# Another order of an expert's intermediate units, so that its second weight matrix arrives in larger pieces

## The chip, the cores and the metric

The kernel runs on one core of a Trainium2 chip, in one launch. The metric is the time on the device in microseconds (us).

## The reference, cut to what matters

Two blocks follow each other on 256 tokens of 1024 features, in float32. The first has two layers of a mixer (attention, convolution, stick breaking attention) and a mixture of experts; the second has two layers of another mixer. The change is in the experts of the first block:

```
N_EXPERTS = 64; TOP_K = 8; EXPERT_FF = 256          # D_MODEL = 1024, SEQ = 256

def swiglu(x, w1, w3, w2):
    return (jax.nn.silu(x @ w1) * (x @ w3)) @ w2     # w1, w3: 1024 x 256; w2: 256 x 1024

    def expert_block(args):                          # for each block of tokens sent to expert e
        toks, e, wts = args
        out = swiglu(xpad[toks], w1[e], w3[e], w2[e])
        return out * wts[:, None].astype(out.dtype)
```

Each expert has 256 intermediate units: columns of w1 and w3, rows of w2. The sum over the units in the second product may take them in any order.

## The kernel before

SBUF has 128 partitions. The tokens of an expert are handled in blocks of 64 slots, a list of blocks with their experts being made on the chip after the router. Each layer first runs one block per expert and then the extra ones; the loop takes four blocks (`UNROLL`) a turn, as two pairs (`PAIRS`).

For a block `j` TensorE does, in the order that `pair` writes out by hand:
- `gather` (L1186): picks the tokens of the next pair by a product with a one-hot matrix in bf16, in halves, between the other products.
- `block_h` (L1198): the first product. The contraction runs over the 1024 features, `KT` = 8 tiles of 128. The stationary operand is `x_blk`, 128 features by 64 slots; the moving one is the weights in the ring `w13(j)`, for each feature 256 columns of w1 and 256 of w3. With 64 slots only half of the array's columns are used, so the units are split into two halves `g`, which go to two column tiles side by side: tile 0 writes partitions 0 to 63 of `h_bank`, tile 1 partitions 64 to 127. In the bank, columns 0 to 127 are the w1 part and 128 to 255 the w3 part. A float32 product of the program is two instructions in the trace.
- `block_turn` (L1207, L1210, L1212): the activation `act_blk` (slots of both halves on the partitions, 128 units across) is turned by TensorE. Afterwards partition p holds unit p of half 0 in columns 0 to 63, and unit p of half 1 in columns 64 to 127 (`turned`).
- `pair_w2` (L1225): the second product, for the two blocks of a pair on two column tiles: `turned` stationary, `w2_slots` moving, 512 columns, half `f` of the units from the slot's part `f`.
- `pair_add` (L1238): the weighted results, split into three bf16 parts, are added to the tokens' sums in PSUM.

ScalarE makes the sigmoid (L1488) and copies; VectorE multiplies (L1956, L1958) and applies the norm to the gathered tokens (L1948, L1950).

SP issues all weights by DMA: `expert13` (L670) loads w1 and w3 of an expert into a ring slot, with one contiguous piece of 8192 bytes per partition each (the eight features of a partition lie together), and `expert2` (L675) loads w2 into one of four `w2_slots`, which lie in the tensors `slots2`, `qk` and `z`. In the loop SP waits until block_h has read the ring slot of the last turn (`h_done`), issues expert13, then waits until pair_w2 has read the w2 slot (`o_done`, L797), and issues expert2. So each load has about one turn of the loop less its issue delay before it is read.

Of the kernel before, what the change touches and what calls it, by code (L numbers as in the profile page):

```python
# [31 lines left out]
P = 128  # L32
# [15 lines left out]
N_EXPERTS, N_GROUPS, TOPK_GROUPS, TOP_K, FF = 64, 8, 4, 8, 256  # L48
# [382 lines left out]
def first_block(nc, A, K):  # L431


    ds = bass.ds
    with ExitStack() as ctx:
# [103 lines left out]
        for n in (PAIRS * T * P // 2, FF // 2, FF // 2):  # L539
# [13 lines left out]
        w2_slots = [slots2[:, 0], slots2[:, 1], qk[:].rearrange("p t n -> p (t n)").rearrange("p (f n) -> p f n", f=2),  # L553
                    z_flat[:, 0:T * D].rearrange("p (f n) -> p f n", f=2)]
# [10 lines left out]
        for layer in range(DEPTH):  # L565
            chunks = chunks_1(layer)
            for i, (name, reader) in enumerate(chunks):
                s = i % RING
# [91 lines left out]
        def _(sp):  # L660
# [11 lines left out]
                        .then_inc(w13_filled[s], 16)  # L672

            def expert2(l, e, s):
                sp.dma_start(w2_slots[s], A["w2"][ds(l, 1), ds(e, 1)].rearrange("a b (f p) n -> p (a b f) n", p=P))\  # L675
                    .then_inc(w2_filled[s], 16)

            def load(dst, src, loaded):
# [24 lines left out]
            for l in range(DEPTH):  # L703
# [55 lines left out]
                for e in range(UNROLL):  # L759
# [4 lines left out]
                    else:  # L764

                        sp.wait_ge(B[l][before].full, B[l][before].full_at(l))
                    expert13(l, e, e)
                expert2(l, 0, 0)

                sp.wait_ge(sh_done.sem, sh_done.at(l, T))  # L770
                expert2(l, 1, 1)

                sp.wait_ge(parts_ready.sem, parts_ready.at(l))
                expert2(l, 2, 2)
                expert2(l, 3, 3)
                if l + 1 < DEPTH:
# [57 lines left out]
        def _(pe):  # L834
# [41 lines left out]
            for l in range(DEPTH):  # L876
# [195 lines left out]
                for g in range(4):  # L1072
                    bank = begin(("mT", g), l)
                    for j in range(2):
                        for t in range(T):
                            k = 2 * g + j
# [46 lines left out]
                def w13(s):  # L1123
                    return K.slots[s].rearrange("p (i k) n -> p i (k n)", i=2).rearrange("p i (k n) -> p i k n", n=FF)
# [66 lines left out]
                def block_h(it, j):  # L1191


                    pe.wait_ge(w13_filled[j], uses(it, j // 2) * 32)
                    own = slice(j % 2 * SLOTS, (j % 2 + 1) * SLOTS)
                    for k in range(KT):
                        for g in range(2):
                            mm = nc.tensor.matmul(h_bank[g * SLOTS:(g + 1) * SLOTS, 0:FF], x_blk[:, j // 2, k, own],  # L1198
                                                  w13(j)[:, :, k, g * (FF // 2):(g + 1) * (FF // 2)],
                                                  start=(k == 0), stop=(k == KT - 1), skip_group_check=True)  # L1200
                    mm.then_inc(h_done, 1)

# [40 lines left out]
                def pair(it, i, first=False, last=False):  # L1243
                    a, b = 2 * i, 2 * i + 1

                    pe.wait_ge(x_ready, nth(it, b))
                    block_h(it, a)
                    if not last:
                        gather(it, i + 1, 0)
                    if not first:  # L1250

                        pe.wait_ge(o_rest_ready, nth(it, b - 2))
                    block_turn(it, a)
                    block_h(it, b)
                    if not last:
                        gather(it, i + 1, 1)

                    pe.wait_ge(turned_ready, nth(it, a))
                    pe.wait_ge(weight_ready, pairs(it, i))
                    block_turn(it, b)  # L1260
                    if not first:
                        pair_add(it, i - 1)

                    pe.wait_ge(turned_ready, nth(it, b))
                    if not last:

                        pe.wait_ge(x_ready, nth(it, b + 2))
                    pair_w2(it, i)
# [1492 lines left out]
```

## Time and profile before

| | |
|---|---|
| time, median of 3 runs | 2237.6 us |
| lowest and highest | 2233.91 and 2243.11 us |
| the profiled execution | 2242.32 us |
| its span, first to last instruction | 2240.6 us |
| mean granted TensorE clock in it | 0.985 |
| DMA packets, bytes | 165286, 599.13 MB |

The span is the time in which instructions ran; the profiled execution's own time holds 1.7 us more. Engines are called PE (TensorE's products), PEld (its weight loads), DVE (VectorE), ACT (ScalarE), POOL and SP. Durations of matmuls include their way through the array, so instructions that follow each other overlap in the trace; the distance between starts is the rate.

### The profile page before, as it was taken

How to read it: one execution, taken by the hardware profiler on the slowest of the kernel's cores; microseconds unless marked ns; L12 is line 12 of the kernel's file. 1: busy time of each engine (PE TensorE's matmuls, PEld its weight loads, DVE VectorE, ACT ScalarE, POOL GpSimd, SP SyncE). 2: the span in 40 equal slices, each digit the busy share in tenths (PEclk: the TensorE clock that was granted, in tenths of full speed). 3: DMA queues.
4: the chain of work that ended last, by engine and by line, in shares of the span. 5: the costliest groups of instructions: out<-in, count | busy, mean ns of one | idle time of the engine just before them, and what ended most of it. 6: DMA issues, size and time to landing. Idle time of an engine off the chain costs nothing. (4 is left out here: it accounts for less than half of the span.)

```text
span 2240.6 us, 34873 instructions
## 1 busy us (share of the span) xinstructions
PE 2132.4 (95%) x13404; PEld 1232.9 (55%) x13404; DVE 973.5 (43%) x2062; ACT 510.0 (23%) x1077; POOL 59.7 (3%) x143
## 2 busy tenths in 40 slices
PE   5999999899999999979999988999999999799998
PEld 3844444556556565557454445556565565367475
DVE  2673423544444444428634244444444443353153
ACT  2223112122222222223231111222222222113131
POOL 1000002000000000000000030000000000100000
PEclk9999999999999999989999999999999999899999
DMA  9652838699999999845527437999999998531721
GB/s 325 203 206 75 300 113 319 224 385 376 385 378 382 386 379 381 341 179 179 198 105 260 167 130 279 380 382 381 383 378 389 377 386 286 178 111 57 225 69 56
DMA packets 165286, 599.13 MB, mean 267 GB/s; under 512 B 13052, under 2 KB 17760, under 8 KB 130656
## 3 DMA queue, kind: packets, MB, share of 16 engines
q1 hardware_dynamic: 163808, 595.10, 70.7%
q0 software_dynamic: 1408, 3.10, 0.7%
q8 instruction: 44, 0.72, 0.1%
q14 instruction: 26, 0.21, 0.0%
HBM read 597.11 MB, written 1.05 MB: 267 GB/s over the span
## 5 line engine op out<-in xcount | busy, mean ns | idle before, releaser
L1198 PE MATMUL banks<-weight_ring,h_t 128*64 128x256 f32 x4224 | 481.8, 381 | 3.2 <-DVE h_t L1950 3.2
L1198 PEld LDWEIGHTS banks<-weight_ring,h_t 128*64 128x64 f32 x4224 | 298.3, 137 | 174.0 <-issue 38.2
L849 PE MATMUL banks<-weight_ring,h_t 128*128 128x512 f32 x768 | 335.8, 593 | 4.1 <-issue 1.6
L849 PEld LDWEIGHTS banks<-weight_ring,h_t 128*128 128x128 f32 x768 | 145.1, 190 | 187.6 <-issue 182.8
L1976 DVE SCALAR_TENSOR_TENSOR conv_t<-banks,slot_weight,xn 128x512 f32<-128x512 f32 x132 | 99.1, 751 | 293.5 <-ACT xn L1503 293.5
L1186 PEld LDWEIGHTS banks<-z,sp_ 128*128 128x128 bf16 x3168 | 178.8, 98 | 55.8 <-issue 49.3
L1186 PE MATMUL banks<-z,sp_ 128*128 128x128 bf16 x3168 | 201.0, 220 | 4.9 <-DVEq L1940 4.9
L1238 PE MATMUL banks<-xn,conv 128*128 128x512 bf16 x792 | 185.9, 385 | 6.7 <-issue 4.0
L1503 ACT ACTIVATE xn<-banks,slot_weight 128x512 bf16<-128x512 f32 x132 | 90.7, 687 | 342.6 <-PE banks L1225 342.6
L1956 DVE TENSOR_TENSOR z<-banks,z 128x128 f32<-128x128 f32 x132 | 38.5, 292 | 230.0 <-ACT z L1488 230.0
L2209 PE MATMUL banks<-weight_ring,h_t 128*128 128x512 f32 (+2 forms) x384 | 134.1, 509 | 2.9 <-ACTq L2385 2.9
L1238 PEld LDWEIGHTS banks<-xn,conv 128*128 128x128 bf16 x792 | 78.6, 100 | 89.9 <-issue 9.8
L1225 PE MATMUL banks<-slots,conv 128*64 128x512 f32 x544 | 124.2, 598 | 3.1 <-DVE h_t L1950 3.1
L859 PE MATMUL banks<-h_t,weight_ring 128*128 128x256 f32 x512 | 116.3, 391 | 6.1 <-DVEq L1555 4.5
L1948 DVE TENSOR_TENSOR h_t<-banks,mod_col 128x512 f32<-128x512 f32 x132 | 91.4, 692 | 65.2 <-PE banks L1186 65.2
L1225 PE MATMUL banks<-qk,conv 128*64 128x512 f32 x256 | 116.7, 598 | 0.0
L1225 PE MATMUL banks<-z,conv 128*64 128x512 f32 x256 | 116.7, 598 | 0.0
L859 PEld LDWEIGHTS banks<-h_t,weight_ring 128*128 128x128 f32 x512 | 100.4, 197 | 21.1 <-DVEq L1555 4.6
L1488 ACT ACTIVATE z<-banks 128x128 f32<-128x128 f32 x132 | 36.6, 278 | 327.0 <-PE banks L1198 327.0
L2209 PEld LDWEIGHTS banks<-weight_ring,h_t 128*128 128x128 f32 x384 | 69.0, 190 | 63.5 <-issue 58.4
L1602 DVE SCALAR_TENSOR_TENSOR conv<-hpad,vec_t,conv 128x256 f32<-128x256 f32 x240 | 100.3, 480 | 4.7
L1950 DVE TENSOR_TENSOR h_t<-h_t,mod_col 128x512 f32<-128x512 f32 x132 | 91.4, 692 | 9.8
(467 smaller groups left out, 2045.2 us busy)
## 6 DMA issues: line engine op xcount, KB each, us to landing
weight_ring<-in_w SPq DMA_DIRECT2D x264, 1024.0 KB, 10.9
weight_ring<-in_w_in SPq DMA_DIRECT2D x36, 2048.0 KB, 11.5
slots<-in_w SPq DMA_DIRECT2D x68, 1024.0 KB, 8.5
weight_ring<-in_w_mod SPq DMA_DIRECT2D x24, 2048.0 KB, 10.0
qk<-in_w SPq DMA_DIRECT2D x32, 1024.0 KB, 7.0
z<-in_w SPq DMA_DIRECT2D x32, 1024.0 KB, 11.4
weight_ring<-in_w_out SPq DMA_DIRECT2D x8, 2048.0 KB, 7.8
weight_ring<-in_w_in SPq DMA_DIRECT2D x10, 1024.0 KB, 7.7
```

The costliest lines, as they stand in the source:

```text
L849: mm = nc.tensor.matmul(bank[:, 0:cols], stationary[:, k, t * P:(t + 1) * P], w[:, k, 0:cols], start=(k == 0), stop=(k == KT - 1))
L859: mm = nc.tensor.matmul(bank[:, j * SEQ:(j + 1) * SEQ], w[:, k, c * P:(c + 1) * P], K.h_t[:, k, :], start=(k == 0), stop=(k == KT - 1))
L1186: mm = nc.tensor.matmul(x_banks[half][:, kk * P:(kk + 1) * P], xn_parts[:, t, c, half * KT // 2 + kk, :], pick_hot[:, i % PAIRS, t, :], st ...
L1198: mm = nc.tensor.matmul(h_bank[g * SLOTS:(g + 1) * SLOTS, 0:FF], x_blk[:, j // 2, k, own], w13(j)[:, :, k, g * (FF // 2):(g + 1) * (FF // 2)],
L1225: mm = nc.tensor.matmul(o_banks[h][b * SLOTS:(b + 1) * SLOTS, :], turned[:, i, b, f * SLOTS:(f + 1) * SLOTS], w2_slots[2 * i + b][:, f, h ...
L1238: mm = nc.tensor.matmul(y_bank[t][h][:], slot_of[:, i % PAIRS, t * P:(t + 1) * P], o_parts[:, c, h * CHUNK:(h + 1) * CHUNK], start=False, ...
L1503: nc.scalar.activation(o_parts[:, 0, col], o_banks[h][:], ACT.Copy, scale=slot_weight[:, i % PAIRS:i % PAIRS + 1])\
L1602: v.scalar_tensor_tensor(conv[:, c, :], hpad[:, c, k:k + SEQ], w, conv[:, c, :], ALU.mult, ALU.add)
L1948: v.tensor_tensor(x, x_banks[half][:].rearrange("p (k s) -> p k s", k=KT // 2), broadcast(mod_col[:, 3, ks], 2, P), ALU.mult)
L1950: v.tensor_tensor(x, x, broadcast(mod_col[:, 2, ks], 2, P), ALU.add).then_inc(x_ready, 1)
L1976: v.scalar_tensor_tensor(o_rest[:, col], o_banks[h][:], own, o_parts[:, 0, col], ALU.mult, ALU.subtract)\
L2209: mm = nc.tensor.matmul(bank[:, 0:cols], stationary[:, k, t * P:(t + 1) * P], w[:, k, 0:cols], start=(k == 0), stop=(k == KT - 1))
```

## The change

Two edits. `expert2` loads w2 so that partition p gets the rows 2p and 2p + 1 (before: p and 128 + p); these lie together in memory, so each partition has one piece of 8192 bytes instead of two of 4096. To match, the moving operand of `block_h` gives tile `g` every second column, starting at `g`, of the 256 columns of w1 and w3 (before: the columns g * 128 to g * 128 + 127). Partition p of `turned` then holds the units 2p and 2p + 1.

```
             def expert2(l, e, s):
-                sp.dma_start(w2_slots[s], A["w2"][ds(l, 1), ds(e, 1)].rearrange("a b (f p) n -> p (a b f) n", p=P))\
+                sp.dma_start(w2_slots[s].rearrange("p f n -> p (f n)"), A["w2"][ds(l, 1), ds(e, 1)].rearrange("a b (p f) n -> p (a b f n)", f=2))\
                     .then_inc(w2_filled[s], 16)
...
                             mm = nc.tensor.matmul(h_bank[g * SLOTS:(g + 1) * SLOTS, 0:FF], x_blk[:, j // 2, k, own],
-                                                  w13(j)[:, :, k, g * (FF // 2):(g + 1) * (FF // 2)],
+                                                  w13(j)[:, :, k, g::2],
                                                   start=(k == 0), stop=(k == KT - 1), skip_group_check=True)
```

## Rows read from the trace of the kernel before

**Rows 1.** The page's busy time of each engine, share of the span, instructions.

```profile
PE 2132.4 (95%) x13404; PEld 1232.9 (55%) x13404; DVE 973.5 (43%) x2062; ACT 510.0 (23%) x1077; POOL 59.7 (3%) x143
```

**Rows 2.** Windows: us, then PE, PEld, DVE, ACT, POOL busy, PE clock, DMA share, GB/s.

```profile
440.00:935.00 495.00, 495.00 (x4384) 293.43 (x4381) 220.93 (x481) 117.22 (x271) 0.00 (x0) 1.00 0.98 382
1390.00:1900.00 510.00, 507.77 (x4474) 299.95 (x4473) 224.79 (x488) 121.16 (x279) 0.00 (x0) 1.00 0.96 372
```

**Rows 3.** PE's waits from 415 to 940 us: total us, times, longest.

```profile
PE banks L1186 <- DVEq L1940: 2.0, 1, 2.0
PE banks L1198 <- DVE h_t L1950: 1.6, 1, 1.6
PE banks L1225 <- DVE h_t L1950: 1.5, 1, 1.5
```

**Rows 4.** PE's groups in the expert stage: out<-moving,stationary, shapes, count | busy us, mean ns.

```profile
L1198 PE MATMUL banks<-weight_ring,h_t 128*64 128x256 f32 x4224 | 481.8, 381 | 3.2 <-DVE h_t L1950 3.2
...
L1207 PE MATMUL banks<-ident,z 128*128 128x128 f32 x132 | 37.1, 281 | 4.8 <-DVE z L1958 4.8
```

**Rows 5.** Order of time on PE: start us, length us, what, count.

```profile
603.14 3.62 PE L1198 MATMUL banks<-weight_ring,h_t 128*64 128x256 f32 x32
...
619.64 2.54 PE L1198 MATMUL banks<-weight_ring,h_t 128*64 128x256 f32 x22
...
632.66 3.65 PE L1225 MATMUL banks<-slots,conv 128*64 128x512 f32 x16
```

**Rows 6.** Streams of other products: two groups, and four column tiles in order of time.

```profile
L849 PE MATMUL banks<-weight_ring,h_t 128*128 128x512 f32 x768 | 335.8, 593 | 4.1 <-issue 1.6 <-DMA weight_ring<-in_w_in 1.6 <-ACTq L1453 0.9
...
L2236 PE MATMUL banks<-h_t,weight_ring 128*128 128x256 f32 x256 | 56.1, 380 | 0.0
...
137.08 1.92 PE L886 MATMUL banks<-weight_ring,c_act 128*32 128x512 f32 x16
```

**Rows 7.** Transposes by line: ns min/median/max. L870 step 8, L1111 step 2, L992 contiguous.

```profile
L870 PEld LDWEIGHTS banks<-ident,xn x16: 185/192/197, 35.3 to 37.2; 128*128 128x128 f32 x16
L870 PE MATMUL banks<-ident,xn x16: 272/274/278, 35.7 to 37.3; 128*128 128x128 f32 x16
...
L1111 PEld LDWEIGHTS banks<-ident,act_h x4: 196/216/262, 1341.5 to 1342.3; 128*128 128x128 f32 x4
...
L992 PEld LDWEIGHTS banks<-ident,xn x32: 138/140/144, 177.1 to 1121.9; 128*128 128x128 f32 x32
```

**Rows 8.** DMA: packets; L675's issue times and landing; SP's wait; SP in time.

```profile
DMA packets 165286, 599.13 MB, mean 267 GB/s; under 512 B 13052, under 2 KB 17760, under 8 KB 130656
...
L675 SPq DMA_DIRECT2D slots<-in_w x68: 378/384/1545, 402.2 to 1874.9; - x68
...
DMA to landing us min/median/max: 4.9/8.6/14.3
...
SPq L797 <- PE banks L1225: 653.2, 62, 11.6
...
605.84 1.53 SPq L675 DMA_DIRECT2D slots<-in_w  x1
```

**Rows 9.** A window (columns as in rows 2) in which loads queue up.

```profile
1343.00:1345.00 2.00, 1.57 (x8) 1.18 (x9) 0.70 (x5) 0.50 (x2) 0.00 (x0) 1.00 1.05 442
```

More of the change, by code:

```diff
@@ L674, in expert2 @@
             def expert2(l, e, s):
-                sp.dma_start(w2_slots[s], A["w2"][ds(l, 1), ds(e, 1)].rearrange("a b (f p) n -> p (a b f) n", p=P))\
+                sp.dma_start(w2_slots[s].rearrange("p f n -> p (f n)"), A["w2"][ds(l, 1), ds(e, 1)].rearrange("a b (p f) n -> p (a b f n)", f=2))\
                     .then_inc(w2_filled[s], 16)
@@ L1198, in block_h @@
                             mm = nc.tensor.matmul(h_bank[g * SLOTS:(g + 1) * SLOTS, 0:FF], x_blk[:, j // 2, k, own],
-                                                  w13(j)[:, :, k, g * (FF // 2):(g + 1) * (FF // 2)],
+                                                  w13(j)[:, :, k, g::2],
                                                   start=(k == 0), stop=(k == KT - 1), skip_group_check=True)
```

## Prediction

> **What bounds the kernel now.** I read the page's busy line first [rows 1]: TensorE is busy for 2132.4 us of the 2240.6 us span, so whatever TensorE does is the candidate. The change touches only the expert stage, so the next view is the windows of that stage [rows 2]. From 440 to 935 us (first layer) TensorE is busy for 495.00 of 495 us, from 1390 to 1900 us (second layer) for 507.77 of 510 us, at a granted clock of 1.00. The same rows show the DMA engines at 98% and 96% of their time, moving 382 and 372 GB/s. Two resources look full; which of them sets the pace must come from the waits. TensorE's waits from 415 to 940 us [rows 3] are three, 5.1 us together, all for VectorE and all at the stage's start. None is for a DMA. The transfers are close to full because they are asked for at just that rate, not because TensorE stands waiting for them.
>
> The groups by line [rows 4] show what TensorE does there. The first product (L1198) is 4224 instructions, 481.8 us; L1207 runs once per block of 64 slots, so there are 132 blocks and 32 instructions of L1198 in each. They go in twos: the two halves of the columns are computed on two column tiles side by side. I call two such instructions a step: 4224 / 2 = 2112 steps, and 481.8 us / 2112 = 228 ns a step, tails included. In the order of time [rows 5] 32 instructions take 3.62 us; without the last one's own length (381 ns), 15 intervals share 3.24 us, 216 ns each. A pair of blocks takes 619.64 - 603.14 = 16.5 us, all of it TensorE's work.
>
> **The change part by part.**
>
> *Moving operand of L1198.* Instruction count, columns per instruction (256), weights loaded and PSUM columns written stay. What changes is that each tile reads every second float of the w1 and w3 rows (a step of 8 bytes) instead of 128 floats in a row. No moving operand of the trace of before reads with a step, so this price is unknown and must be bounded.
> - From below: can a step get shorter? L2236 [rows 6] is the same 256 columns on the whole array, one stream: 56.1 us / 256 = 219 ns. The two tiles (216 to 228 ns) already run at the pace of one stream, so the columns set it, not the reads. Bound: 0.
> - From the reads as they are: how much can the moving side deliver? L886 runs four column tiles with four different streams of 512 floats. Its 16 instructions take 1.92 us [rows 6]; without the last one's 0.59 us, three intervals share 1.33 us, 443 ns for four streams at once. L849 needs 335.8 us / 768 = 437 ns for one stream of the same length. So four contiguous streams cost no more than one. Two streams with a step of two walk over as many bytes per ns as four contiguous ones (each walks over twice what it uses). By this row they fit: price 0.
> - From above: a stepped read does cost something elsewhere. The weight load of the transposes at L870 (a step of 8 floats) takes 192 ns at the median, that of L992 (contiguous, the same 128x128 floats) 140 ns [rows 7]; L1111, with the very step of 2, has a minimum of 196 and a median of 216 ns. L870's own matmuls take 272 to 278 ns, so it was not the clock. That is 52 ns for 128 columns, 0.41 ns a column. Such a load takes 0.41 ns more, but the moving side is slower to begin with: from 380 ns at 256 columns (L2236) to 593 ns at 512 (L849) [rows 6], 0.83 ns a column. If a stepped read can deliver one float each 0.83 ns, the load drops to exactly that and the moving read does not notice. If instead the same 0.41 ns is added per moving column, a step costs 256 x 0.41 = 105 ns more, 2112 x 0.105 = 222 us. If each column took twice its 0.83 ns, it would be 213 ns a step, 450 us.
>
> I take 0. The two rows with the same kind of read and the same rate (L886 for the sum of the streams, L870 for one stream at its slowest) both leave room; the 222 and 450 us need a limit that neither row shows. It is at the edge, though: both fit without slack that I can see.
>
> The Trainium skill, "SBUF — State Buffer", section "Specifications (TRN2)", says that the memory has 16-byte lines and needs at least two accesses in a line for full bandwidth. Floats with a step of two have exactly two in a line, so by that rule the sum stays at 0 for one stream; the page says nothing of two streams that share a line. L870's step of eight, with one access in a line, is slowed by the 52 ns above, which agrees with it; L1111's step of two is slowed as much, which speaks against it. The sums of this text don't use it.
>
> *Layout of w2.* 132 transfers of 1 MB change from two pieces of 4096 bytes per partition to one of 8192. The page counts 130656 packets under 8 KB [rows 8]; 132 x 256 = 33792 of them become 16896 larger ones. TensorE reads the same SBUF addresses as before. Landing can get quicker: now 8.6 us at the median and 14.3 at most. Who would see it? SP issues the second transfer of a pair at 605.84 us, and its slot is read by L1225 at 632.66 us [rows 5, 8]: 26.8 us later, 12.5 us more than the slowest landing. SP itself waits 653.2 us for L1225 to free slots [rows 8], so issue time saved there (0.38 us a transfer) is hidden behind TensorE too. Worth: 0. The cover is TensorE's work of 16.5 us a pair; were it gone, the value is bounded by the rate. From 1343 to 1345 us, when transfers queue with nothing to hold them, 442 GB/s show [rows 9] against the stage's 382: were w2's third of the stage's 1005 us to go from the one rate to the other, 335 x (1 - 382/442) = 45 us. But TensorE's idle time in the two windows is 2.2 us in all, so not even that could be taken.
>
> *Both together.* Units 2n and 2n+1 now stand on the two tiles, and after the turn partition n holds them, which is where w2's rows 2n and 2n+1 now lie. ScalarE's and VectorE's work between (sigmoid, products, turn) keeps shape and place: 0.
>
> Sum: 2242.3 us (the profiled execution: span 2240.6 and 1.7 around it) + 0 + 0. That execution is 0.2% above the median of the three runs shown (2237.6), so against the median I say 2237.5.
>
> **The rivals.**
> 1. *A stepped moving read is slower by what a stepped weight load is slower.* Place: L1198, where TensorE has no idle time to hide it. For it: L1111 and L870 [rows 7]. Against: the moving side needs only half the load's rate. Price 222 us: 2460 us. It decides from 11.2 us (0.5%) / 2112 = 5.3 ns a step on. This is the case on the other side.
> 2. *The two tiles' streams get in each other's way*, because they now read even and odd floats of the same few bytes at the same time, and go one after the other. For it: nothing in the trace has two tiles on neighbouring floats. Against: L886's four streams. Price 213 ns a step, 450 us: 2688 us.
> 3. *The transfers set the pace after all*, in a way that a wait list can hide: faster, up to 45 us: 2192 us by rate, 2235 by the idle time that there is. For it: 98% DMA share. Against: no wait for a DMA in the stage.
> 4. *The transfer doesn't change* (the pieces are cut again on their way): same time, as forecast; only the packet counts would tell.
>
> **How the numbers follow.** About 0.5% (11 us) is what a measurement of this kernel can tell from no change. Forecast, no change: 0.82 (rival 4 is within it). Rival 1: 0.08; rival 2: 0.05; a small fixed price of some ns a step, between 0.5% and 1%: 0.02. Rival 3, beyond 0.5%: 0.03. So faster 0.03, same 0.82, slower 0.15. Range: 2228 to 2252 us. It holds the forecast with the spread of the runs and the small fixed price; rivals 1 and 2, 0.13 together, and rival 3's 0.03 lie outside, since nothing fills the gap up to them.
>
> **What the profile of after would show.** Right: L1198 still near 481.8 us with 4224 instructions of 381 ns; the pair of blocks still 16.5 us; the stage's windows still without TensorE idle; about 16900 packets fewer and the count under 8 KB lower by 33800, while the stage's GB/s stay, its DMA share doesn't rise and w2's landing is no later. Rival 1 or 2: L1198's mean per instruction above 381 ns, its group above 700 us, the DMA share of the stage down to 70 to 80%, because the same bytes are asked for over a longer time. Rival 3: a pair of blocks shorter than 16.5 us with L1198 unchanged. The prediction is wrong if the rate that L886 shows for four tiles doesn't carry over to stepped reads.

## The result, and the profile after

The change made the kernel slower by 1.1%: median 2261.36 us against 2235.9 us in the same session (4 runs each, 2259.91 to 2264.13 against 2233.91 to 2243.11), a ratio of 1.0106 with a 95% interval of 1.0082 to 1.013. The interval means 18 to 29 us more. The forecast was 2237.5 us, with 2228 to 2252 as its range; the time lies above the range.

The profiled execution of the changed kernel took 2260.18 us with a span of 2258.4 us, at a mean granted clock of 0.987. That is only 17.9 us more than the profiled execution before (2242.32 us, clock 0.985), which was one of the longer ones of its kernel. So the sizes below are read from groups of the expert stage, where the windows of both show a granted clock of 1.00, and not from the two spans. The page:

```profile
span 2258.4 us, 34873 instructions
PE 2152.0 (95%) x13404; PEld 1233.1 (55%) x13404; DVE 973.1 (43%) x2062; ACT 509.9 (23%) x1077; POOL 59.8 (3%) x143
...
DMA packets 148390, 599.13 MB, mean 265 GB/s; under 512 B 13052, under 2 KB 17760, under 8 KB 96864
```

Against [rows 1] only TensorE's busy time moved, by 19.6 us (the others by at most 0.4); the number of instructions is the same. The packets fell by 16896 and those under 8 KB by 33792, just as 132 transfers of half as many pieces should [rows 8]. So the transfer did change, and rival 4 falls.

The groups by line (columns as in rows 4) say where TensorE's time went:

```profile
L1198 PE MATMUL banks<-weight_ring,h_t 128*64 128x256 f32 x4224 | 504.8, 389 | 3.2 <-DVE h_t L1950 3.2
L849 PE MATMUL banks<-weight_ring,h_t 128*128 128x512 f32 x768 | 335.8, 593 | 4.3 <-issue 1.7 <-DMA weight_ring<-in_w_in 1.6 <-ACTq L1453 0.9
L1186 PE MATMUL banks<-z,sp_ 128*128 128x128 bf16 x3168 | 202.6, 221 | 4.9 <-DVEq L1940 4.9
```

L1198 went from 481.8 to 504.8 us [rows 4]: 23.0 us over 2112 steps, 10.9 ns a step. One instruction went from 381 to 389 ns. L849, which the edits don't touch, has the same 335.8 us as in [rows 6]. All of TensorE's busy time grew by less than L1198's 23.0 us because some other groups took a little less in this execution (L1119 14.6 us against 16.8).

In the order of time (columns as in rows 5), a pair of blocks of the changed kernel:

```profile
606.63 3.79 PE L1198 MATMUL banks<-weight_ring,h_t 128*64 128x256 f32 x32
...
612.06 3.85 PE L1198 MATMUL banks<-weight_ring,h_t 128*64 128x256 f32 x32
...
623.48 3.79 PE L1198 MATMUL banks<-weight_ring,h_t 128*64 128x256 f32 x32
```

The 32 instructions take 3.79 us instead of 3.62 [rows 5], and the pair 623.48 - 606.63 = 16.85 us instead of 16.5: 0.35 us for each of 66 pairs, 23 us. Nothing absorbs it, as the windows show (columns as in rows 2):

```profile
440.00:935.00 495.00, 495.00 (x4307) 288.66 (x4305) 216.88 (x472) 114.71 (x265) 0.00 (x0) 1.00 0.95 373
1390.00:1900.00 510.00, 510.00 (x4437) 297.19 (x4434) 223.71 (x487) 118.28 (x274) 0.00 (x0) 1.00 0.95 374
```

TensorE is as full as in [rows 2], but in the first 495 us it issues 4307 instructions instead of 4384. The transfers move 373 GB/s where they moved 382, because the same bytes are asked for over a longer time. SP's answer for the w2 slots is the other side of it:

```profile
SPq L797 <- PE banks L1225: 708.9, 62, 12.0
```

It waits 708.9 us for TensorE to free them, where it waited 653.2 [rows 8]. The w2 loads also land a little sooner, 8.3 us after their issue at the median and 12.2 at most, against 8.6 and 14.3 [rows 8]. The loads have got more slack, and the kernel is slower.

### The profile page after: what moved, and what is told of

It reads as the page before. It is cut to its first block and busy times, and to the rows that moved or that the text cites. A ratio compares the mean times of both kernels' runs of the same rounds, so it can differ in the third digit from the quotient of the medians.

```text
span 2258.4 us, 34873 instructions
## 1 busy us (share of the span) xinstructions
PE 2152.0 (95%) x13404; PEld 1233.1 (55%) x13404; DVE 973.1 (43%) x2062; ACT 509.9 (23%) x1077; POOL 59.8 (3%) x143
## 5 line engine op out<-in xcount | busy, mean ns | idle before, releaser
L1198 PE MATMUL banks<-weight_ring,h_t 128*64 128x256 f32 x4224 | 504.8, 389 | 3.2 <-DVE h_t L1950 3.2
L1198 PEld LDWEIGHTS banks<-weight_ring,h_t 128*64 128x64 f32 x4224 | 299.4, 134 | 193.1 <-issue 38.2
L849 PE MATMUL banks<-weight_ring,h_t 128*128 128x512 f32 x768 | 335.8, 593 | 4.3 <-issue 1.7
L849 PEld LDWEIGHTS banks<-weight_ring,h_t 128*128 128x128 f32 x768 | 145.1, 190 | 187.8 <-issue 182.9
## 6 DMA issues: line engine op xcount, KB each, us to landing
weight_ring<-in_w_in SPq DMA_DIRECT2D x36, 2048.0 KB, 11.5
z<-in_w SPq DMA_DIRECT2D x32, 1024.0 KB, 11.1
```

What stands on the lines that cost most here:

```text
L849: mm = nc.tensor.matmul(bank[:, 0:cols], stationary[:, k, t * P:(t + 1) * P], w[:, k, 0:cols], start=(k == 0), stop=(k == KT - 1))
```

## The experiments

A step below is two instructions side by side on two column tiles (one instruction where the whole array is used, four on four tiles). Each bench is one execution, so its small differences rest on the 96 steps of a pattern and on patterns that were repeated.

### One edit at a time

`cols_only` has only the edit of the first product, `w2_only` only that of the load.

```
# cols_only
-                                                  w13(j)[:, :, k, g * (FF // 2):(g + 1) * (FF // 2)],
+                                                  w13(j)[:, :, k, g::2],
# w2_only
-                sp.dma_start(w2_slots[s], A["w2"][ds(l, 1), ds(e, 1)].rearrange("a b (f p) n -> p (a b f) n", p=P))\
+                sp.dma_start(w2_slots[s].rearrange("p f n -> p (f n)"), A["w2"][ds(l, 1), ds(e, 1)].rearrange("a b (p f) n -> p (a b f n)", f=2))\
```

> The first product's tiles take even and odd units, w2 stays in two pieces of 4096 bytes (so units and rows of w2 no longer match and the output is another). Theory A, the stepped moving read costs some 11 ns a step of two instructions: all of the change's loss is here, 2112 x 0.0109 = 23 us, ratio 1.0105, the group of L1198 near 505 us. Theory B, the larger pieces of w2 slow what TensorE reads beside them: ratio 1.000, L1198 near 482 us. If both take part, the ratio lies between.

> w2 in one piece of 8192 bytes per partition, the first product's tiles take contiguous halves as before (units and rows of w2 don't match, so the output is another). Theory A: ratio 1.000 and L1198 at 482 us, since no TensorE instruction waits for a DMA. Theory B: ratio 1.01, L1198 near 505 us. A gain of over 0.3% would mean that the transfers did set part of the pace before.

Measured: `cols_only` 2265.19 us against 2239.63 us, ratio 1.012 (1.0097 to 1.0142). `w2_only` 2239.52 us, ratio 0.9998 (0.9986 to 1.001). The group of L1198, first of `cols_only`:

```profile
L1198 PE MATMUL banks<-weight_ring,h_t 128*64 128x256 f32 x4224 | 504.8, 389 | 3.2 <-DVE h_t L1950 3.2
```

and of `w2_only`, with its first window (columns as in rows 2):

```profile
L1198 PE MATMUL banks<-weight_ring,h_t 128*64 128x256 f32 x4224 | 481.8, 381 | 3.2 <-DVE h_t L1950 3.2
...
440.00:935.00 495.00, 495.00 (x4384) 293.31 (x4382) 220.94 (x480) 117.23 (x271) 0.00 (x0) 1.00 0.97 382
```

The whole loss belongs to the stepped columns: the intervals of `cols_only` and of the changed kernel overlap, and both hold the 23.0 us of L1198. The larger pieces alone neither cost nor gain anything that these runs can tell (0.9986 to 1.001). SP's wait at L797 is 707.3 us in `cols_only` and 655.7 in `w2_only`, so its growth, too, comes from the slower TensorE. Theory A holds, B falls.

### The read patterns by themselves

`bench_quiet` issues, on TensorE alone, 96 steps of each of 25 read patterns, the kernel's own slices among them, and `bench_dma` the same while 230 loads run. Each pattern is a loop like this one:

```
            for r in range(REPEATS):            # 6
                for k in range(KT):             # 8
                    for g in range(2):
                        mm = nc.tensor.matmul(psum[g * 64:(g + 1) * 64, 2, 0:256], x_k[:, k, g * 64:(g + 1) * 64], a13[:, :, k, g::2], start=(k == 0), stop=(k == KT - 1), skip_group_check=True)
```

> TensorE alone, no transfers beside it: 96 steps (192 instructions) of each of 25 read patterns, one after the other; nothing of the reference is computed. Theory A1, a price per stepped instruction or per column of each stream: pattern 7 (one tile, step 2) and pattern 9 (whole array, step 2) are slower than 6 and 8 by 5 to 11 ns an instruction. Theory A2, the two tiles' streams get in each other's way because they lie on neighbouring floats: patterns 7 and 9 cost nothing, 2 costs 11 ns a step, 3 (both even) and 4 (different slots) differ from 2. Per column against per instruction: at 512 columns (18 against 17) the extra is 22 ns in the first case, 11 in the second; at 128 columns (20 against 19) 5.5 or 11. If what counts is the number of 16-byte lines walked over, steps 4 and 8 cost more than step 2 and runs of four floats (11) cost nothing. Theory C, transfers into SBUF collide with the longer walks: here no pattern costs anything.

> The same 25 patterns while 230 transfers of 1 MB run beside them. Theories A1 and A2: the same step times as in bench_quiet within 1 ns. Theory C, transfers collide with the reads: the stepped patterns 2, 3, 4, 13 cost 11 ns a step here and nothing in bench_quiet.

Measured, the groups by line of `bench_quiet` (out<-moving,stationary; shapes; count | busy us, mean ns): contiguous halves (L75, and L195 once more at the end), step 2 even and odd (L80), both even (L85); tile 0 contiguous beside tile 1 at step 2 (L95); one tile alone, contiguous (L100) and step 2 (L105); whole array contiguous (L110) and step 2 (L115); four tiles contiguous (L175) and step 2 (L180); steps 3, 4 and 8 (L140, L145, L150); 512 columns contiguous (L155) and step 2 (L160); runs of two floats in turn (L120) and of four (L125).

```profile
L75 PE MATMUL banks<-wa,x_tokens 128*64 128x256 f32 x192 | 20.9, 379 | 0.0
...
L80 PE MATMUL banks<-wa,x_tokens 128*64 128x256 f32 x192 | 21.9, 388 | 0.0
...
L85 PE MATMUL banks<-wa,x_tokens 128*64 128x256 f32 x192 | 21.9, 388 | 0.0
...
L95 PE MATMUL banks<-wa,x_tokens 128*64 128x256 f32 x192 | 22.3, 388 | 0.0
...
L100 PE MATMUL banks<-wa,x_tokens 128*64 128x256 f32 x192 | 41.6, 379 | 0.0
...
L105 PE MATMUL banks<-wa,x_tokens 128*64 128x256 f32 x192 | 43.5, 387 | 0.0
...
L110 PE MATMUL banks<-wa,x_tokens 128*128 128x256 f32 x96 | 21.0, 380 | 0.0
...
L115 PE MATMUL banks<-wa,x_tokens 128*128 128x256 f32 x96 | 21.9, 387 | 0.0
...
L175 PE MATMUL banks<-wa,x_tokens 128*32 128x256 f32 x384 | 20.9, 379 | 0.0
...
L180 PE MATMUL banks<-wa,x_tokens 128*32 128x256 f32 x384 | 21.9, 387 | 0.0
...
L140 PE MATMUL banks<-wa,x_tokens 128*64 128x256 f32 x192 | 32.8, 509 | 0.0
...
L145 PE MATMUL banks<-wa,x_tokens 128*64 128x256 f32 x192 | 43.8, 633 | 0.0
...
L150 PE MATMUL banks<-wa,x_tokens 128*64 128x256 f32 x192 | 44.4, 639 | 0.0
...
L155 PE MATMUL banks<-wa,x_tokens 128*64 128x512 f32 x192 | 41.4, 592 | 0.0
...
L160 PE MATMUL banks<-wa,x_tokens 128*64 128x512 f32 x192 | 43.4, 611 | 0.0
...
L120 PE MATMUL banks<-wa,x_tokens 128*64 128x256 f32 x192 | 22.0, 388 | 0.0
...
L125 PE MATMUL banks<-wa,x_tokens 128*64 128x256 f32 x192 | 20.9, 379 | 0.0
...
L195 PE MATMUL banks<-wa,x_tokens 128*64 128x256 f32 x192 | 20.9, 379 | 0.0
```

Readings:
- Step 2 costs 21.9 - 20.9 = 1.0 us for 96 steps, 10.4 ns a step: the kernel's 10.9.
- It is no matter of the neighbour. Both tiles on the even floats (L85), tiles on different slots (21.9 us), the whole array with one stream (L115) and four tiles (L180) cost the same, and one tile alone pays 9.9 ns for each instruction (L100, L105). Theory A2, the forecast's rival 2, falls.
- One pattern doesn't fit "each stream for itself": a contiguous stream beside a stepped one (L95) takes 22.3 us, 0.4 us more than two stepped ones, and the same in `bench_dma`. Why, no run here shows.
- It grows with the columns: 43.4 - 41.4 = 2.0 us at 512, 11.2 - 10.7 = 0.5 us at 128. It is no fixed price of an instruction.
- It grows steeply with the step up to 4 and then stops: 32.8, 43.8 and 44.4 us at steps 3, 4 and 8.
- Runs of four floats, every second one left out, are free; runs of two cost what step 2 costs.
- In `bench_dma` every pattern has the same time within 0.1 us, while the transfers move 413 GB/s. The loads ran out at about 591 us, so the last patterns, the four tiles (from 588.1 us) among them, had next to none beside them; all the others did. Theory C falls.

The window of `bench_dma` that says so (us, then PE, PEld, DVE, POOL busy, PE clock, DMA share, GB/s):

```profile
50.00:600.00 550.00, 550.00 (x3796) 324.28 (x3796) 0.00 (x0) 0.00 (x0) 1.00 0.99 413
```

What unites them: without the last one's own length, 95 intervals share the time of 96 steps. I take the memory in lines of 16 bytes, four floats each, and count those that a stream enters. At step 4 an interval is (43.8 - 0.63) / 95 = 454 ns, 1.77 ns for each of 256 floats, and each float is in 16 bytes of its own. At step 3, (32.8 - 0.51) / 95 = 340 ns; four floats lie in three such lines, so 192 lines at 1.77 ns. At step 2, (21.9 - 0.39) / 95 = 226 ns; 128 lines at 1.77 ns. Contiguous, 216 ns: 64 lines would need 113 ns, and now the columns set the time at 0.84 ns each. So the stream needs 1.77 ns for each 16-byte line that it enters (at step 8 it is 1.80), and two columns need 1.69 ns: a step of two floats is too slow by that small difference.

### The alignment, and the dose inside the kernel

`fours` gives tile g every second run of four units, `step4` reads every fourth float.

```
# fours
-                                                  w13(j)[:, :, k, g * (FF // 2):(g + 1) * (FF // 2)],
+                                                  w13(j)[:, :, k, :].rearrange("p i (m g c) -> p i m g c", g=2, c=4)[:, :, :, g, :],
# step4
-                                                  w13(j)[:, :, k, g * (FF // 2):(g + 1) * (FF // 2)],
+                                                  K.slots[j].rearrange("p k n -> p (k n)")[:, k * FF + g:k * FF + 4 * FF:4],
```

> In the first product tile g takes every second run of four units (16 bytes) instead of every second unit; w2 as before (units and rows of w2 don't match, so the output is another). Line theory, the price is for 16-byte lines walked over per column: ratio 1.000, L1198 at 482 us, because each line that is fetched gives four floats as before. Pattern theory, any moving operand that is not one run per matrix costs 11 ns a step: ratio 1.010, L1198 at 505 us.

> In the first product each tile reads every fourth float over four rows of features (256 columns as before, other values, so the output is another). Line theory, with the bench's step time of 43.8 against 20.9 us for 96 steps: 238 ns more a step, 2112 x 0.238 = 504 us, time near 2740 us, ratio 1.225, L1198 near 980 us. If the kernel around hides part of it: less. Theory of a fixed price per stepped instruction: ratio 1.010 as with step 2.

Measured: `fours` 2238.57 us against 2239.0 us, ratio 1.0001 (0.9986 to 1.0015). `step4` 2767.78 us, ratio 1.236 (1.2321 to 1.2398). The group of L1198 in `fours`:

```profile
L1198 PE MATMUL banks<-weight_ring,h_t 128*64 128x256 f32 x4224 | 481.8, 381 | 3.2 <-DVE h_t L1950 3.2
```

and in `step4`, with the group that counts its blocks and a window (columns as in rows 2):

```profile
L1198 PE MATMUL banks<-weight_ring,h_t 128*64 128x256 f32 x4288 | 992.2, 630 | 4.8 <-DVE h_t L1950 4.8
...
L1207 PE MATMUL banks<-ident,z 128*128 128x128 f32 x134 | 37.4, 279 | 7.1 <-DVE z L1958 7.1
...
440.00:935.00 495.00, 493.54 (x2987) 209.61 (x3009) 153.04 (x333) 81.59 (x187) 0.00 (x0) 1.00 0.66 262
```

`fours` is free inside the kernel too: the price isn't for the pattern but for the lines. `step4` has 134 blocks instead of 132: 66 in the first layer as before and two more in the second, whose router sees other values. Its step takes 992.2 us / 2144 = 463 ns against 228, 235 ns more; the bench said 238. L1198 grows by 510.4 us of the 528.8. Of the other 18.4 us some 9 are an estimate of the rest of one more pair (16.5 us without its two runs of L1198, 3.62 us each [rows 5]); what is left isn't taken apart. The price of a step is of the size that rival 2 named (213 ns), and the window shows what a large price looks like: TensorE full, the DMA share down to 0.66.

`bench_lines` moves the runs off the lines and tries the weight loads:

> TensorE alone, 24 patterns, 96 steps each (48 or 96 instructions where one pass or one tile is said); nothing of the reference is computed. Line theory (about 1.75 ns for each 16-byte line that a stream enters, against 0.83 ns for each column, the larger of the two setting the time): runs of four that lie astride two lines (4) cost like step 2 (0.87 ns a column, 21.9 us) although runs of four on the lines (3) are free (20.9 us); runs of eight off the lines (6) are free; two floats in a line with six left out (7) cost like step 2, two floats astride two lines (8) like step 4 (43.8 us); steps 5 and 6 cost like step 4. bf16 at step 2 costs 4% and at step 4 twice. Run-length theory (the price follows how long a run is): 4 is free as 3 is, 8 costs as 7, steps 5 and 6 cost like step 4. Weight loads: transposes at step 2, 4 and 8 take the same 190 ns against 140 contiguous; ordinary weight loads at step 2 the 190 ns that they take now.

Measured, its groups by line: contiguous (L84), runs of four on the lines (L94) and two floats off (L99), eights two floats off (L109), two floats in a line with six left out (L114), the same two floats astride two lines (L119), steps 5 and 6 (L134, L139), bf16 contiguous (L144), at step 2 (L149) and step 4 (L154).

```profile
L84 PE MATMUL banks<-wa,x_tokens 128*64 128x256 f32 x192 | 20.9, 379 | 0.0
...
L94 PE MATMUL banks<-wa,x_tokens 128*64 128x256 f32 x192 | 20.9, 379 | 0.0
...
L99 PE MATMUL banks<-wa,x_tokens 128*64 128x256 f32 x192 | 21.9, 387 | 0.0
...
L109 PE MATMUL banks<-wa,x_tokens 128*64 128x256 f32 x192 | 21.8, 386 | 0.0
...
L114 PE MATMUL banks<-wa,x_tokens 128*64 128x256 f32 x192 | 22.3, 391 | 0.0
...
L119 PE MATMUL banks<-wa,x_tokens 128*64 128x256 f32 x192 | 43.7, 632 | 0.0
...
L154 PE MATMUL banks<-flat_b,xb 128*64 128x512 bf16 x96 | 22.0, 633 | 0.0
```

Two floats with six left out cost 22.3 us inside a line and 43.7 us across two; runs of four are free on the lines and cost 1.0 us off them. Steps 5 and 6 take 44.4 and 43.7 us, as 4 does. bf16 behaves alike (10.6, 11.1 and 22.0 us), though its columns go by in half the time (10.6 us for 48 steps of 512): at step 4 it has two values in a line, as floats have at step 2, but wants them twice as fast, so the line sets the time: 22.0 us / 48 / 256 lines = 1.79 ns. So it is the 16-byte line. One expectation missed clearly: runs of eight at two off, which the mean over their lines would let through, cost 0.9 us. The pair inside a line missed by a little: 22.3 us where a step of 2, with as many lines, takes 22.0 in this bench (L124).

For the weight loads the bench takes products of 128 columns whose stationary operand is stepped. With ordinary loads 96 of them take 10.9 us contiguous, 11.5 at step 2 and 23.0 at step 8; one load lasts 192, 196 and 335 ns at the median. Transposes take 5.4 us for 48 contiguous, 5.9 at steps 2 and 4 and 5.5 at step 8; one load lasts 140, 209, 209 and 193 ns. So the load of a transpose pays about the same for every step, unlike the moving read, whose price grows with the step up to 4.

`bench_runs` takes up the miss:

> TensorE alone, 96 steps of each pattern, nothing of the reference is computed. Open: why runs of eight floats that lie off the 16-byte lines cost as much as a step of two. Theory M, a stream needs the larger of 1.75 ns and 0.83 ns per float used for every line it enters, with no averaging over lines: per 256 columns runs of 4 at 2 off cost 10 ns, runs of 8 at 2 off 5 ns, of 16 2.5 ns, of 32 1.3 ns, so 21.9, 21.4, 21.15, 21.0 us for 96 steps; at 1 or 3 off the short line has one float and the price doubles or more (runs of 4: one line of one float at 1.75 and one of three at 2.5, 1.06 ns a float, 26.5 us). Theory J, a fixed price for each matrix whose stream has any short line: 21.8 us for runs of 4 to 64 alike. Theory Q, a short queue evens neighbouring lines out: at 1 and 3 off runs of 4 cost the same 21.9 us as at 2 off, since two lines still serve four floats. Runs of 4 on the lines cost nothing whether 4 or 12 floats are left out.

| run length, floats off the line | 96 steps, us |
|---|---|
| contiguous: 0; 1, 2 or 3 | 20.9; 21.0 |
| 4: 1; 2; 3 | 25.8; 21.9; 26.1 |
| 8: 1; 2; 3; 4 | 22.4; 22.0; 22.6; 20.9 |
| 16: 1; 2; 3 | 21.7; 21.3; 21.7 |
| 32, 64, 128: 2 | 21.3; 21.1; 21.0 |
| 2: 0; 1 | 22.0; 22.2 |
| 4 with 12 left out: 0; 2 | 21.2; 22.6 |
| step 2 | 22.8 |

Theory J falls (the price fades with longer runs), and so does Q (one or three off costs five times two off for runs of four). Theory M fits runs of four (26.5 us said, 25.8 and 26.1 measured): there a line entered for one float is not made good by the line after it. Its sizes are not right for longer runs, and they miss on both sides: runs of eight at two off cost 22.0 us where it says 21.4, while at one off its rule, worked out in the same way, gives 23.7 and 22.4 was measured. How far neighbouring lines help each other stays open. The last three patterns of this bench are not used: the last of them, step 2, took 22.8 us where the other benches have 21.9 and 22.0, at an unchanged 388 ns an instruction. So the expectation that runs of four are free with 12 left out as well (21.2 us) stays open, too.

### What the larger pieces are worth when nothing covers them

> Only w2 loads, four phases of 60 transfers of 1 MB, four in flight: two pieces of 4096 bytes a partition, one of 8192, and again both; nothing of the reference is computed. If the larger pieces carry more when transfers are the limit, phases 2 and 4 are shorter than 1 and 3: by 1 to 3% from the small fall of the DMA share in the changed kernel. If they carry the same, all four phases are equal within 0.5% and the edit could not have helped even a kernel that waits for its loads.

The windows of the four phases (us, then PE, PEld, DVE, POOL busy, PE clock, DMA share, GB/s):

```profile
20.00:160.00 140.00, 1.08 (x2) 0.29 (x2) 0.07 (x1) 0.00 (x0) 1.00 1.03 410
180.00:310.00 130.00, 0.00 (x0) 0.00 (x0) 0.00 (x0) 0.00 (x0) 1.00 1.01 422
330.00:470.00 140.00, 0.00 (x0) 0.00 (x0) 0.00 (x0) 0.00 (x0) 1.00 1.03 410
490.00:620.00 130.00, 0.00 (x0) 0.00 (x0) 0.00 (x0) 0.00 (x0) 1.00 1.01 422
```

410 GB/s in pieces of 4096 bytes, 422 in pieces of 8192, both times: 3% more. The gain of the load edit is real, but the kernel asks for 382 GB/s, less than the smaller pieces already carry. The 442 GB/s of the forecast's bound of 45 us [rows 9] are those of a window of 2 us; with the 422 that last, the same sum gives 32 us.

## Why the prediction was wrong, and where it was right

- **What bounds the kernel** was right: TensorE in the expert stage, with the transfers close to full but never waited for. `w2_only` (0.9998) and `bench_loads` show it from both sides, and `cols_only` shows the reverse: 23 us more on TensorE appear in the time in full. The load edit was worth 0 as said, and rivals 3 and 4 had nothing behind them.
- **The price of the moving operand** is the step that failed: taken as 0, it measured 10.9 ns a step, 23.0 us. Comparing the rate of a stepped read with the rate of the columns was the right kind of bound, and I stopped too early at it. The text saw that the stepped read would need exactly the rate that the columns ask for and found no slack, and yet priced the misfit at 0, though 5.3 ns a step, 2.4% of one, was enough to decide. With 1.77 ns a line against 1.69 ns for two columns, "just fits" was 5% short, and 5% of a 482 us group is twice what a measurement can tell.
- **L886 was the wrong witness.** I argued from the sum over streams: four contiguous ones walk over as many bytes as two stepped ones. The limit is one of each stream: one, two and four streams at step 2 all cost the same (21.9 us in each case). A row with four contiguous streams cannot show it. This is the condition that the prediction itself gave for being wrong: L886's rate doesn't carry over to stepped reads.
- **L870 and L1111 were the wrong upper witnesses**, too: they are loads of a transpose, which slow down by about as much at step 2 (209 ns) as at 8 (193 ns, against 140), while the moving read pays 5% at step 2 and 110% at step 4.
- **The rivals.** Rival 1 had the place and the point of decision right (5.3 ns a step) and the size ten times too large. The case that came true, "a small fixed price of some ns a step", was named and given 0.02; it isn't fixed, and at 10.9 ns a step and 23.0 us it is 1.03%, just past the 1% at which that case ended. The range followed the chances and so ended too low: between a price of 0 and one of 105 ns a step nothing was known, and "nothing fills the gap" was a guess. It didn't even hold what it says it holds: its top, 2252 us, is 0.65% above the forecast, while the small fixed price reached up to 1%, 2260 us.
- **The rule of the Trainium skill** ("SBUF — State Buffer", "Specifications (TRN2)": 16-byte lines, two accesses in a line for full bandwidth) is right in its mechanism, as L94 against L99 and L114 against L119 show. Its threshold is right within 5%: two floats a line reach 0.88 ns a column, not 0.84.

## What to carry to other kernels

When a matmul reads its moving operand with a step, count the 16-byte lines per column: up to one line for four floats (on the lines) was free here, one for two cost 5%, one for each float doubled the time and more. If units must be dealt out to tiles, deal them in aligned runs of four. Dealing fours pairs unit n with unit n + 4, though, so the two rows of w2 that a partition needs would no longer lie together, and the one piece of 8192 bytes would be lost. And before a load is made more efficient at another engine's expense, look for a wait on it: here there was none to win, so the exchange could only lose. When a bound comes out as "just fits", price the misfit at a few per cent of the group instead of at 0.

## What the runs showed of the hardware that I had not expected

- A stream of TensorE needs 1.77 ns for each 16-byte line at steps 2, 3 and 4 alike (1.80 at step 8). At step 2 one, two and four column tiles and the whole array pay alike, and up to two tiles do so with 413 GB/s of transfers beside them as without.
- Where runs start off the lines, the short lines at their ends cost time: runs of four floats starting one float off a line take 25.8 us where two off take 21.9 and none off 20.9. The price fades with longer runs (128 floats at two off: 21.0).
- The load of a transpose lasts 209 ns at steps 2 and 4, 193 at step 8 and 140 contiguous; an ordinary weight load lasts 192 ns contiguous, 196 at step 2 and 335 at step 8.
- Loads of 1 MB with one piece of 8192 bytes per partition run at 422 GB/s, with two of 4096 at 410.
